# One order for all expert units, a mixer second half in two parts, and context adds on column groups

## What is computed

```
h = rmsnorm(x) * (1 + sc_m) + sh_m;  proj = h @ w_in          # mixer, input half
attn = attention(rope(norm(q)), [k_cache, k], [v_cache, v])    # 8 heads of 64, 2 key heads
hy   = x0 * (fftconv(x1 * v) + skip * x1 * v);  sg = chunk_gmlp(...)
x = x + g_m * (concat[attn, hy, sg] @ w_out)                   # mixer, second half
h = rmsnorm(x) * (1 + sc_f) + sh_f
q = h @ wq; s = q . keys           # per head 2 x 128 scores
idx, gate = top 16 of the 16 x 16 sums of the two top 16s; softmax
a = gelu(h . peer_u[idx]);  x = x + g_f * sum_e gate_e a_e peer_v[idx_e]
```

## Time and profile before

| | |
|---|---|
| timed runs, us | 4668.66, 4685.74, 4687.51 |
| profiled execution, span of its instructions, us | 4627.7 |
| profiled execution's own time outside the span | not given by the profile |
| TensorE, VectorE, ScalarE, GpSimd busy | 74%, 64%, 23%, 62% |
| gathers of expert rows | 1342.34 MB of 1486.11 MB, 321 GB/s over the span |
| mean granted TensorE clock | 0.935 of full |

### The profile page before, as it was taken

One profiled execution on the slowest core, in us unless ns is written; L12 is line 12 of the kernel. 1 busy time (PEld: TensorE's weight loads), 2 busy tenths in 40 slices (PEclk: granted clock), 3 DMA queues, 4 the chain that ended last, 5 costly groups with the idle time before them and its releaser, 6 DMA issues.

```text
span 4627.7 us, 39193 instructions
## 1 busy us (share of the span) xinstructions
PE 3424.7 (74%) x9648; PEld 1527.8 (33%) x9648; DVE 2972.4 (64%) x6847; ACT 1072.4 (23%) x2261; POOL 2880.2 (62%) x2564
## 2 busy tenths in 40 slices
PE   8778886678778776677676978946666766667777
PEld 2644653122333332222222546422222222222222
DVE  0279999545566555666664889986666665656662
ACT  1332321121232212121122323211212112121222
POOL 0034555456667676777773545657777777777775
PEclk9889898899999899999998989969999999999999
DMA  7468788989899998999995977879999999999998
GB/s 286 162 224 294 256 298 284 351 314 360 332 354 353 335 370 323 360 376 346 354 377 170 331 257 249 328 258 354 361 355 339 356 360 333 363 341 346 371 370 295
DMA packets 392139, 1486.11 MB, mean 321 GB/s; under 512 B 44108, under 2 KB 45838, under 8 KB 375888
## 3 DMA queue, kind: packets, MB, share of 16 engines
q0 software_dynamic: 368640, 1342.34, 79.5%
q1 hardware_dynamic: 23248, 141.13, 8.0%
HBM read 1480.42 MB, written 2.88 MB: 321 GB/s over the span
## 4 chain that ended last, share of the span: by engine, by line
DMA 32%; PE 25%; DVE 17%; issue 17%; POOL 6%; ACT 3%; POOLq 0%; SPq 0%; DVEq 0%; ACTq 0%
DMA rows_ring<-in_peer_v,idx 19%; DMA rows_ring<-in_peer_u,idx 12%; PE psum L825 12%; POOL rows_ring L548 6%; DVE rows_ring L1366 5%; DVE mix L1380 4%; PE psum L648 4%; PE psum L604 3%; PE psum L770 1%; PE psum L635 1%; DVE small L1288 1%; DMA ring<-in_ada 1%; PE psum L782 1%; PE psum L811 0%; PE psum L597 0%
## 5 line engine op out<-in xcount | busy, mean ns | idle before, releaser
L825 PE MATMUL psum<-rows_ring,diag 128*128 128x512 f32 x4096 | 2067.1, 634 | 901.0 <-DMA rows_ring<-in_peer_v,idx 723.9
L1366 DVE SCALAR_TENSOR_TENSOR rows_ring<-rows_ring,area 128x1024 f32<-128x1024 f32 x1280 | 1562.7, 1225 | 957.9 <-DMA rows_ring<-in_peer_u,idx 935.2
L548 POOL DMA_INDIRECT rows_ring<-in_peer_u,idx x1280 | 1419.7, 1109 | 1084.5 <-DVE rows_ring L1366 431.9
L548 POOL DMA_INDIRECT rows_ring<-in_peer_v,idx x1280 | 1460.3, 1141 | 637.4 <-issue 287.1
L825 PEld LDWEIGHTS psum<-rows_ring,diag 128*128 128x128 f32 x4096 | 730.6, 196 | 2192.0 <-issue 950.6
L1057 ACT ACTIVATE diag<-ident,wts 128x128 f32<-128x128 f32 x1024 | 381.7, 397 | 1515.1 <-PE psum L825 1514.3
L648 PE MATMUL psum<-area,ring 128*128 128x128 f32 (+1 forms) x1344 | 381.8, 443 | 17.1 <-ACT area L919 17.1
L1380 DVE SCALAR_TENSOR_TENSOR mix<-rows_ring,wts,mix 128x1024 f32<-128x1024 f32 x254 | 326.2, 1284 | 8.7 <-DMA rows_ring<-in_peer_v,idx 7.6
L648 PEld LDWEIGHTS psum<-area,ring 128*128 128x128 f32 x1344 | 213.4, 198 | 188.2 <-issue 185.1
L604 PE MATMUL psum<-ring,csil 128*2 128x512 f32 x384 | 176.4, 615 | 21.5 <-DMA ring<-in_ada 21.5
L1049 ACT ACTIVATE acts<-dots 128x16 f32<-128x16 f32 x80 | 17.3, 216 | 555.8 <-DVE rows_ring L1366 555.6
(11 more groups left out here) (174 smaller groups left out, 2473.6 us busy)
## 6 DMA issues: line engine op xcount, KB each, us to landing
ring<-in_ada SPq DMA_DIRECT2D x48, 1024.0 KB, 7.1
ring<-in_win SPq DMA_DIRECT2D x32, 1024.0 KB, 7.7
rows_ring<-in_peer_u,idx POOLq DMA_INDIRECT x1280, 6.1
rows_ring<-in_peer_v,idx POOLq DMA_INDIRECT x1280, 6.2
ring<-in_wout SPq DMA_DIRECT2D x16, 1024.0 KB, 6.7
ring<-in_wq SPq DMA_DIRECT2D x16, 1024.0 KB, 7.3
ring<-in_dft SPq DMA_DIRECT2D x12, 1024.0 KB, 7.7
xT<-in_xT_in SPq DMA_DIRECT2D x1, 2560.0 KB, 15.2
```

Of the source, the lines that this page charges most:

```text
L548: pool.indirect_dma_start(row(table, k), None, (peer_u, peer_v)[table], bass.IndirectOffsetOnAxis(ap=idx[n][:, k:k + 1], axis=0)).then_inc ...
L825: m = pe.matmul(acc[:, b, :], diag[:, k % 4, :], row(1, k)[:, b * 512:(b + 1) * 512], start=False, stop=False)
L1366: dve.scalar_tensor_tensor(out=row(0, k), in0=row(0, k), scalar=1.0, in1=h_tok[GROUPS[grp][1]][:, bass.ds(t * D_MODEL, D_MODEL)], op0=ALU. ...
```

## The change

- There is one unit sequence over all 80 units without a first or last step of a group (`step_jobs(v)`, v from 0 to 81): dots of unit v, u fetches four rows ahead (`down`), v fetches in groups of four (`up`), adds of unit v - 2 (groups 2 and 3) and v - 1 (groups 0 and 1), picks of unit v + 1. No loops are left, and GpSimd follows the same list. `close` only copies the sum; `back` transposes it in two halves into PSUM bank 2, in the second step after.
- The latent mixer's second half (attention output, w_out, norm, wq, keys) runs in two parts, tile 0 and then tiles 1 to 3, each part loading w_out, wq and keys anew. Tile 0's units go beside the second part. `ROOM` has new weights.
- Context adds go to TensorE. The unit's indices and weights are turned so that one gather brings 4 slots of 32 tokens; a 128x32 stationary matrix (`spread`) adds them into 32 PSUM partitions, four such matmuls per bank in four column groups. The four rows of a group come free together.
- Attention: two score banks instead of three, plain transposes, v as the moving operand (64 columns), normalisation once a tile on the output rows, then transposes back.
- `mod`: the four matmuls of a half go to four column groups of one bank, after one matmul with zeros; `modT` adds the four rows up.
- `stage` is gone: picks work on the scores in place. Mixer jobs have 5 PSUM banks instead of 6.

```diff
+PARTS = (((0, 1), (1, LAT_TILES)), ((0, 1),))
...
+    a, b = PARTS[st][part]
+    first, last = 8 * a, 8 * b - 1
+    jobs = [("fence", l, st, 2 * part), ("as", l, st, first)]
+    for n in range(first, last + 1):
+        jobs += [("as", l, st, n + 1)] if n < last else []
+        jobs += [("ao", l, st, n // 8 - 1)] if n >= first + 8 and n % 8 == 1 else []
+        jobs += [("at", l, st, n)] + ([("av", l, st, n - 1)] if n > first else [])
+        jobs += [("an", l, st, n // 8 - 1)] if n > first and n % 8 == 0 else []
+    return jobs + [("av", l, st, last), ("an", l, st, b - 1), ("ao", l, st, b - 1), ("fence", l, st, 2 * part + 1)]
...
+ROOM = {"mod": 56, "modT": 5, "rms": 100, "f1": 25, "f2": 25, "f3": 12, "hf": 35, "qk": 69, "vt": 54, "hs": 9, "rot": 9,
+        "ck": 2, "ko": 2, "hy": 69, "su": 69, "ut": 8, "sp": 8, "df": 35, "cv": 75, "as": 13, "at": 7, "av": 7, "an": 0,
+        "ao": 6, "wo": 52, "wq": 52, "tok": 5, "ka": 9, "kb": 9, "fence": 0}
...
+PICK_AT = ((0, 1), (2, 3), (4, 5), ())
+QUADS = TOPK // 4
+
+
+UNIT = [(grp, u) for grp, n in enumerate(UNITS) for u in range(n)]
+
+
+def step_jobs(v):
+
+
+    jobs = []
+
+    def unit(kind, w, n):
+        if 0 <= w < len(UNIT):
+            jobs.append((kind, *UNIT[w], n))
+
+    for p in range(QUADS):
+        parts = list(PICK_AT[p])
+        for i in range(4):
+            k = 4 * p + i
+            unit("dot", v, k)
+            unit("down", v + (k + ROWS) // TOPK, (k + ROWS) % TOPK)
+            if i == 0 and 0 < v <= len(UNIT) and GROUPS[UNIT[v - 1][0]][1] == C_ and p < 2:
+                unit(("turn", "places")[p], v - 1, 0)
+            if v % PEER_HEADS == 1 and v > PEER_HEADS:
+                if (p, i) == (2, 0):
+                    unit("back", v - 2, 0)
+                elif (p, i) == (2, 3):
+                    unit("back", v - 2, 1)
+            if i == 1:
+                m, g = (v - 2, p + 2) if p < 2 else (v - 1, p - 2)
+                unit("add", m, g)
+                if g + 1 == QUADS and m % PEER_HEADS == PEER_HEADS - 1:
+                    unit("close", m, 0)
+                m, g = (m, g + 1) if g + 1 < QUADS else (m + 1, 0)
+                unit("up", m, g)
+                unit("spread", m, g)
+            if i >= 2 and len(parts) > i - 2:
+                unit("pick", v + 1, parts[i - 2])
+    unit("weigh", v, 0)
+    unit("gexp", v + 1, 0)
...
+_first = [("pick", 0, 0, p) for p in range(PICK_PARTS)] + [("gexp", 0, 0, 0)] + [("down", 0, 0, k) for k in range(ROWS)]
+_steps = [_job for _v in range(len(UNIT) + 2) for _job in step_jobs(_v)]
+ORDER, _taken = input_jobs(0, C_) + output_jobs(0, C_, 0) + _first, 0
...
+    end = _steps.index(upto)
+    ORDER += weave(mixer, _steps[_taken:end])
+    _taken = end
...
-    ORDER += weave(mixer_jobs(_l, L_), expert_jobs(_c, range(UNITS[_c] + 1)))
+    stretch(input_jobs(_l, L_) + output_jobs(_l, L_, 0), ("pick", _g, 0, 0))
+    stretch(output_jobs(_l, L_, 1), ("pick", _g, PEER_HEADS, 0))
     if _l + 1 < DEPTH:
+        stretch(input_jobs(_l + 1, C_) + output_jobs(_l + 1, C_, 0), ("pick", _g, 3 * PEER_HEADS, 0))
+        _end = ("back", _g, UNITS[_g] - 1, 1)
+        ORDER += _steps[_taken:_steps.index(_end) + 1]
+        _taken = _steps.index(_end) + 1
+ORDER += _steps[_taken:]
...
+            def fetch_v(grp, u, g):
+                v = UNIT0[grp] + u
+                if GROUPS[grp][1] == C_:
+                    pool.wait_ge(s["place_ready"], turn_of(grp, u) + 1)
+                for j in range(ROWS):
+                    r = v * TOPK + 4 * g + j
+                    if r >= ROWS:
+                        pool.wait_ge(s["v_free"], r + 1 - ROWS)
+                    if GROUPS[grp][1] == C_:
+                        c = QUADS * j + g
+                        at = turned_idx[turn_of(grp, u) % IDX_PLACES][:, c:c + 1]
+                    else:
+                        at = idx[v % IDX_PLACES][:, 4 * g + j:4 * g + j + 1]
+                    pool.indirect_dma_start(row(1, j), None, peer_v, bass.IndirectOffsetOnAxis(ap=at, axis=0)
+                                            ).then_inc(row_landed[1][j], 16)
+
+            for kind, grp, u, p in ORDER:
+                if kind == "down":
+                    fetch_u(grp, u, p)
+                elif kind == "up":
+                    fetch_v(grp, u, p)
...
+                    if half == 0:
+                        pe.matmul(g[:, 0:512], zeros[:], w[:, 0:512], start=True, stop=False)
                     for j in range(4):
-                        m = pe.matmul(g[0:2, 0:512], csil[:, 4 * half + j, :], w[:, j * 512:(j + 1) * 512],
-                                      start=(half == 0 and j == 0), stop=(half == 1 and j == 3))
+                        m = pe.matmul(g[32 * j:32 * j + 2, 0:512], csil[:, 4 * half + j, :], w[:, j * 512:(j + 1) * 512],
+                                      start=False, stop=(half == 1))
...
+            def turn_round(grp, u):
+
+                v, q = UNIT0[grp] + u, turn_of(grp, u)
+                pe.wait_ge(s["w_ready"], v + 1)
+                turned_free(("turn", grp, u, 0))
+                for j in range(4):
+                    for a in range(4):
+                        m = pe.matmul(turned[32 * a:32 * a + 32, j, :, :], ident[:, 32 * j:32 * j + 32],
+                                      turn[v % IDX_PLACES][:, :, 4 * a:4 * a + 4], start=True, stop=True)
+                m.then_inc(s["turn_mm"], 1)
...
+            def add(grp, u, g):
+
+                n = (UNIT0[grp] + u) * QUADS + g
+                first, last = u % PEER_HEADS == 0 and g == 0, u % PEER_HEADS == PEER_HEADS - 1 and g == QUADS - 1
+                if first and n:
+
+                    pe.wait_ge(s["acc_read"], tile_of(grp, u))
+                if GROUPS[grp][1] == C_:
+                    pe.wait_ge(s["diag_ready"], 4 * (n + 1))
+                    for j in range(ROWS):
+                        pe.wait_ge(row_landed[1][j], 16 * (n + 1))
                     for b in range(2):
-                        m = pe.matmul(acc[:, b, :], diag[:, k % 4, :], row(1, k)[:, b * 512:(b + 1) * 512], start=False, stop=False)
-                    m.then_inc(s["v_free"], 1)
-
-            def close_tile(grp, tile):
-                if GROUPS[grp][1] == L_:
-                    for b in range(2):
-                        m = pe.matmul(acc[:, b, :], zeros[:], cos_sin[:, 0, :], start=False, stop=True)
-                    m.then_inc(s["acc_mm"], 1)
-
-                    pe.wait_ge(s["acc_read"], latent_tile(grp, tile) + 1)
+                        for j in range(ROWS):
+                            m = pe.matmul(psum[32 * j:32 * j + 32, b, :], spread[:, n % 4, j, :], row(1, j)[:, b * 512:(b + 1) * 512],
+                                          start=first, stop=last)
+                    m.then_inc(s["v_free"], 4)
                 else:
-
-                    pe.wait_ge(s["v_free"], (tile + 1) * PEER_HEADS * TOPK + ROWS)
-                for k in range(KC):
-                    m = pe.transpose(acc[:, k // 4, k % 4 * P:k % 4 * P + P], out_chunk(GROUPS[grp][1], k), ident[:])
+                    for j in range(ROWS):
+                        pe.wait_ge(s["diag_ready"], 4 * n + j + 1)
+                        pe.wait_ge(row_landed[1][j], 16 * (n + 1))
+                        for b in range(2):
+                            m = pe.matmul(acc[:, b, :], diag[:, j, :], row(1, j)[:, b * 512:(b + 1) * 512],
+                                          start=first and j == 0, stop=last and j == ROWS - 1)
+                        m.then_inc(s["v_free"], 1)
...
```

582 lines of the change are left out of this document (276 added, 306 removed).

## The result

The changed kernel took 4703.63 us (median of 9 runs), the kernel before, run beside it, 4675.63 us (median of 9): ratio 1.0059, interval 1.0036 to 1.0082. The forecast was 4611 us. So the changed kernel took the same time twice, the kernel before did not; it is slower by 0.6% or by nothing, and in no case faster.

The account below looks back on a forecast made before the run. It took VectorE as the bound for context units beside the latent mixer, gathers for units alone. Stretch times summed to 4553 us against the 4627.7 span; that 75 off a 4686 median gave 4611 us, range 4460 to 4715.

Parts of the forecast that it names:

- The largest of DMA, TensorE and VectorE: Units beside the mixer: a stretch takes its busiest resource's time plus an allowance for what doesn't overlap; first stretch 435 us.
- The context round: Four context v rows freed together: issue, landing and adds cycle in 12.5 us, 50 us a unit instead of 46.
- stretch 4: Layer 0 units with no mixer beside them, 10.6 steps: nine at 46.3 us and 1.6 context steps at 52, 500 us.
- The price of the context adds: Context adds on TensorE: eight matmuls in four column groups take 1.8 us together, 7 us a unit.
- Rival C: Mixed stretches: adds queue on TensorE and hold GpSimd, 70 us a unit, 4874 us in all; chance 0.15.
- That stretch is bound by the gathers: Latent units alone, 3489 to 3873 us before: DMA 95% busy, 16.8 MB a unit, 48 us at 349 GB/s.
- Rival B: Gathers bind everywhere: mixed stretches reach their DMA sums, 1548 us instead of 1725, 4434 us in all; chance 0.20.
- The span and the median: Whole kernel: the 75 us saved on the profiled span was taken off a median 58 us above it.
- The 15th weigh, at about 900 us: Sign to look for: VectorE under 70% and DMA over 88% until the 15th unit's weights, at about 900 us.
- rival D: TensorE column groups run one by one: 260 us more work beside the mixer, 4711 us in all; chance 0.08.
- stretch 3: Sixteen units beside layer 1's context mixer: nothing there bound by what changes, 890 us (870 to 920).
- Rival E: Units alone: the rate stays at 48 us a unit through bursts of v, 4672 us in all; chance 0.12.

Follow-up runs that it names:

- e5: Changed kernel with the context adds back on VectorE, no turning; ratio to the kernel before 0.9996.
- e3: Changed kernel with context rows added on TensorE like latent ones, by full-width diagonal multiplies without turning; ratio to the kernel before 1.0084.
- l_after: Changed kernel with gathers of 64 numbers a row instead of 1024, sums wrong; one run, 4479.98 us.
- e10: Changed kernel with nothing interleaved, each stretch's mixer steps first and then its units; 5427.91 us, ratio to the kernel before 1.1567.
- e12: Changed kernel with every v row, context too, fetched, added by diagonal multiplies on TensorE and freed one at a time; 4645.49 us, ratio to before 0.9899.
- e7: Kernel before with only the modulation matmuls put on four column groups; ratio to the kernel before 0.99.
- e11: Changed kernel with context adds on VectorE, latent rows one at a time except first-tile units, which use column groups in fours; ratio to before 1.0116.
- e1: Changed kernel with the latent mixer's second half back in one part; ratio to the kernel before 1.0159.
- e4: Changed kernel with the latent second half in one part and latent v rows fetched and added one at a time; ratio to the kernel before 1.005.
- e9: Kernel before with modulation on column groups and layer 1's first picks moved between layer 0's last adds; ratio to the kernel before 0.9895.

## Why the prediction was wrong

By its own steps, forecast and measured in the profile after, in us: head 211, 213; steps 0 to 6 435, 474; 7 to 14 455, 469; 15 to 30 890, 896; 10.6 steps 500, 518; 5.4 steps 380, 418; 8 steps 455, 468; 25 alone 1157, 1169; tail 70, 64. The sum is 4553 against 4689, 136 short.

- *"The largest of DMA, TensorE and VectorE"* was the wrong rule for a mixed stretch, and this is the step that failed: +39, +14, +38, +13. In none of them was an engine of the changed kernel full (76% at most in the context stretches, 83% beside tiles 1 to 3, DMA 84%), and changing one engine's work moved them little: VectorE (e5 keeps it busy 146 us longer in each context stretch, and they are 18 and 16 us shorter), TensorE (e3: 111 and 106 us more, 8 shorter and 18 longer), DMA (l_after: 4 to 10% shorter with a sixteenth of the bytes). Mixer and units do overlap, by 150 to 200 us in each (e10). The rest shows in the traces as waits of engines for each other: GpSimd waited 147 us of 474 for the dots and 59 for the adds, TensorE 88 us for the rows of those adds, with the mixer's products behind them. That these waits come from the places of dots and adds in the common order is my reading; no run moved them.
- *The context round* of 12.5 us, which I allowed in stretch 4 only, takes 14.2 to 14.6 alone. I had 4.6 for issuing, 6.2 for landing and 1.7 for the adds; the round at 707 us has 5.4 (0.3 between gathers was missing), 5.2, 3.2 (the lower clock) and 0.8 until the next issue. It isn't what made stretch 4 long: of its +18, 13 lie in nine latent steps (430 for 417) and 5 in the 1.6 context steps. Whether it lengthens the stretches beside the mixer, as I thought after e10, stays open: e12 shortened the round and filled TensorE at once.
- *The price of the context adds* was too low: 3.0 us in the mean for eight products, 12 a unit, where I took 1.8 and 7.
- *Rival C* is half right. GpSimd does wait for the adds, 5.4 us a time in the first stretch (11 waits for L897), and the mixed stretches took 1829 us for 28.4 units, a quarter step of 16.1 us, so a wait of 3.6 over 12.5, just over the 3.4 from which C turned the result. But its price of 70 us a unit was too high (64 in the mean), and GpSimd's larger wait is for dots in every one of these stretches. My sign for C, adds as the largest wait beside tiles 1 to 3 with DMA under 80%, did not appear: dots 95 us, adds 34, DMA 84%.
- *"That stretch is bound by the gathers"* saw one of two limits: GpSimd's issuing, 32 times 1.12 + 0.3 us, gives the same 46 us without the bytes. That the number came out (46.3 forecast, 46.6 measured) is part luck: within tiles a unit took 46.3 to 46.8 and not 45.5, and across a tile's end 46.8 to 48.1, where I had added 6. Of the 44 us that the units alone save against e7, half lie at the tile ends and half within the tiles. Rival B fell: the mixed stretches took 1829 us, not 1548.
- *The span and the median.* I added 58 us between profile and median. A timed run is about 2 us above its span (4691.12, the fastest, for 4689.3); before's profile was an unusually quick execution. The sum's own base was right for that execution; 44 of the 136 us cancel there (58 against the 14 that the changed kernel's median lies above its profile), and 93 are left, 4704 for 4611.
- *"The 15th weigh, at about 900 us"* contradicts the sum, which puts it at 1101. It came at 1156, with DMA at 76 and 84% on the way and not over 88%.
- *Right:* the head within 2 us; four column groups do run together (zeroing and 8 products in 2.85 us where I took 2.6), so rival D fell; the seam, with no gap of over 2 us between gathers from 2470 to 2560; stretch 3; the tail. Rival E fell as well, at 46.6 us a unit. The drain that the Trainium skill (TensorEngine Tiling (Array Packing), Key Properties) puts on a change of tiling mode no run isolates: in e11 mode changes, bundles and a lower clock come together.

Put together: the modulation is worth 1%, the units alone some 44 us, the split 0.8% to 1.6% with what it gives back behind the context units already taken off (without it 8-32 took 1285 us in e1 and 1246 in e4, against 1338). Against them stand the bursts of four, 0.3% to 1.9%, and something that no run isolates: e4, with neither split nor latent bursts but with modulation, single sequence, attention and column-group adds, is 0.5% slower than before, though the first two gains are worth some 2%. The one sequence, the new weights of `ROOM` and the new form of attention were never tested alone. Nor was an order tried in which VectorE takes the dots sooner, which the waits of e12 point to.

## What to carry to other kernels

Where two chains share engines in one fixed order, the fullest engine gives only a lower bound: taking work off it can give nothing. A cheaper form that frees ring places in bundles can lose more than it saves (e11), so try it with places freed one by one. An engine or DMA at 95% may only stand beside another limit at the same place: one run with short transfers tells. Set two variants against each other on one chip at one time, and more than once: 0.6% here came and went with the occasion.

## What the runs showed of the hardware

- A gather of 128 rows occupied GpSimd 0.93 to 1.99 us (e10) with 0.3 us between two. Its mean was 1.12 us with 64 numbers a row (l_after) and 1.03 to 1.10 with 1024 (changed kernel), and 32 of them made 46 us in both.
- Four column groups of TensorE with 32 columns ran beside each other: 8 fp32 products of 512 columns in 1.90 us, against 7.03 us in one group.
- The granted clock fell where TensorE mostly waited: 0.56, near the lower of its two levels of 1.2 and 2.4 GHz, in units that kept it 25% busy, where eight adds in column groups took 3.2 to 3.6 us. In the changed kernel the same adds took 1.92 us right behind other work of TensorE and 3.3 to 3.64 mostly where it had waited before them.
- Within a tile, units in hardware loops took 47.9 and 48.1 us (14 units each of e7 and e9), written-out ones of the same kernels 46.7 and 46.8 (6 units each).
- The kernel before had medians of 4676 to 4704 us on six occasions; the changed one, with no loops, 4703.6 and 4703.7.
